# Second attention's filling: half of the output product by seven products of quarters, added straight to the residual rows

## The reference, cut to what matters

```python
def even_layer(h, ..., w_out):
    proj = h @ w_in + b_in
    m_cols, n_cols = jnp.split(proj, [MLSTM_COLS], axis=-1)
    ya = mlstm_branch(m_cols, f_bias, conv_w, conv_b, head_norm)
    yb = nsa_branch(n_cols, q_norm, k_norm, ck_pos, ck_w1, ck_w2, cv_pos, cv_w1, cv_w2)
    return jnp.concatenate([ya, yb], axis=-1) @ w_out
...
    x = x + y.astype(x.dtype)
```

## Time and profile before

| | us |
|---|---|
| median of 3 timed executions | 1676.92 |
| profiled execution, its own time | 1677.36 |
| its span, first to last instruction | 1675.4 |
| TensorE matmuls busy | 1658.8 (99%) |
| VectorE busy | 881.0 (53%) |
| ScalarE busy | 384.7 (23%) |
| GpSimd busy | 205.2 (12%) |

### The profile page before, as it was taken

The page is one execution under the profiler, slowest core; times in us unless marked ns, Lnnn a source line. Parts: engine busy times, 40 slices in busy tenths (PEclk is TensorE's granted clock), DMA queues, the critical chain, the costliest instruction groups (busy, mean ns, idle before and its releaser), DMA issues.

```text
span 1675.4 us, 20036 instructions
## 1 busy us (share of the span) xinstructions
PE 1658.8 (99%) x7754; PEld 1009.6 (60%) x7754; DVE 881.0 (53%) x1497; ACT 384.7 (23%) x690; POOL 205.2 (12%) x267
## 2 busy tenths in 40 slices
PE   9999999999999999999999999999999999999999
PEld 5887888885434343333434456688866654667664
DVE  3755745674523232322325446776756645677663
ACT  3122212002100000010002203331145524544530
POOL 2333410001100000000001000000225510000000
PEclk9999999999999999999999999999999999999999
DMA  7313113245899999999997123213220022212101
GB/s 284 126 57 120 51 51 135 101 175 210 311 422 425 428 426 426 427 427 427 426 428 285 31 104 100 76 58 127 108 101 1 1 76 74 78 50 86 66 1 50
DMA packets 28001, 308.12 MB, mean 184 GB/s; under 512 B 4415, under 2 KB 4703, under 8 KB 10112
## 3 DMA queue, kind: packets, MB, share of 16 engines
q1 hardware_dynamic: 21456, 288.70, 42.6%
q0 software_dynamic: 6448, 18.10, 3.1%
HBM read 306.06 MB, written 4.19 MB: 185 GB/s over the span
## 4 chain that ended last, share of the span: by engine, by line
PE 93%; DVE 3%; DMA 2%; issue 0%; ACT 0%; POOL 0%; DVEq 0%; SPq 0%; ACTq 0%
PE ps L449 89%; PE ps L452 5%; DMA arena<-in_w 2%; DVE arena L1284 2%; DVE arena L1295 0%; POOL small L2967 0%; DVE arena L1311 0%; DVE small L1299 0%; ACT HT L2525 0%; DVE arena L1289 0%; ACT arena L2525 0%; DVE wring L1284 0%; DVE arena L1315 0%; DVE arena L1299 0%; DVE small L1311 0%
## 5 line engine op out<-in xcount | busy, mean ns | idle before, releaser
L449 PE MATMUL ps<-arena 128*64 128x512 f32 (+12 forms) x2484 | 528.4, 394 | 3.6 <-DVE arena L1307 1.2
L449 PEld LDWEIGHTS ps<-arena 128*64 128x64 f32 (+4 forms) x2484 | 251.0, 156 | 219.7 <-issue 208.6
L449 PE MATMUL ps<-wring,arena 128*64 128x512 f32 (+2 forms) x1048 | 345.0, 564 | 0.0
L1284 DVE TENSOR_TENSOR arena<-ps,arena 128x512 f32<-128x512 f32 (+1 forms) x196 | 134.2, 684 | 381.9 <-PE ps L449 229.1
L449 PE MATMUL ps<-wring,HT 128*128 128x512 f32 (+1 forms) x880 | 311.0, 505 | 4.8 <-ACT HT L2525 3.2
L449 PEld LDWEIGHTS ps<-wring,HT 128*128 128x128 f32 x880 | 163.3, 190 | 122.5 <-issue 110.0
L449 PE MATMUL ps<-HT,wring 128*128 128x512 f32 (+2 forms) x656 | 222.1, 501 | 0.0
L2525 ACT ACTIVATE arena<-ps 128x512 f32<-128x512 f32 (+4 forms) x143 | 80.7, 564 | 592.5 <-PE ps L452 303.8
L449 PE MATMUL ps<-wring 128*128 128x256 f32 x864 | 195.8, 380 | 0.0
L449 PEld LDWEIGHTS ps<-wring,arena 128*64 128x64 f32 (+1 forms) x1048 | 131.4, 151 | 87.3 <-issue 82.5
L449 PEld LDWEIGHTS ps<-wring 128*128 128x128 f32 x864 | 162.3, 190 | 24.2 <-issue 2.6
(11 more groups left out here) (125 smaller groups left out, 1002.7 us busy)
## 6 DMA issues: line engine op xcount, KB each, us to landing
wring<-in_w SPq DMA_DIRECT2D x47, 2048.0 KB, 21.3
wring<-in_dense SPq DMA_DIRECT2D x38, 2048.0 KB, 8.3
arena<-in_w SPq DMA_DIRECT2D x35, 2048.0 KB, 20.4
HT<-in_w SPq DMA_DIRECT2D x12, 2048.0 KB, 17.9
arena<-in_rows POOLq DMA_DIRECT2D x29, 256.0 KB, 3.9
wring<-in_dense SPq DMA_DIRECT2D x2, 1024.0 KB, 5.4
H<-in_x SPq DMA_DIRECT2D x4, 512.0 KB, 6.5
arena<-in_relb POOLq DMA_DIRECT2D x8, 256.0 KB, 9.0
```

The source lines that it names most:

```text
L449: return nc.tensor.matmul(o, l, r, start=start, stop=stop, skip_group_check=True)
L1284: done(nc.vector.tensor_tensor(o, a, b, op), tell)
```

## The change

The 16 pieces `e0` go. In their place come 14, named by half of the columns h and product n, in the order of the new table `EIGHTHS` (1, 2, 3, 4, 6, 5, 7): each is one of the seven products of quarters of 256 tokens by 256 inner values by 256 columns, in four matmuls of 256 columns. The quota goes from 0.81 to 0.66 pieces a step; with the 8 pieces `e1` there are 22 pieces instead of 24.

VectorE makes S1 to S4 once (into the space of `y1`, dead by then), behind `nz(6)` and ahead of the loop. For each half h it makes T3 and T2 (`out_sums(h, 3)`), T1 (`out_sums(h, 4)`) and T4 (`out_sums(h, 7)`): T1 and T3 in the place of B11 and B12, T2 and T4 in `kc2`. `out_product` adds each bank to the blocks of `H` that it belongs to: four additions for product 1, one for each other. TensorE waits for `sumw` before products 3 (T2), 4 (T1) and 7 (T4), and for `took` before 6, 5 and 7 (the same bank read before). The wait of a later stage on `suma` goes from 7 to 8, for the one more signal.

```diff
+EIGHTHS = {1: ("a", "A11", "B11"), 2: ("d", "A12", "B21"), 3: ("b", "S2", "T2"), 4: ("c", "S1", "T1"), 6: ("b", "S3", "T3"),
+           5: ("c", "S4", "B22"), 7: ("b", "A22", "T4")}
...
-        FILL_D = softmax_slots([("e0", i, h) for i in range(4) for h in range(2)] + [("e1", i, h) for i in range(4) for h in range(2)],
-                               lambda g: {"e0": 2, "e1": 1}[g[0]], 0.81, NIT + 3, 4)
+        FILL_D = softmax_slots([("e0", h, n) for h in range(2) for n in EIGHTHS] + [("e1", i, h) for i in range(4) for h in range(2)],
+                               lambda g: 1, 0.66, NIT + 3, 4)
...
                     if g[0] == "e0":
-                        _, i, h = g
-                        if p == 0 and i == 0:
+                        _, h, n = g
+                        bank, x, y = EIGHTHS[n]
+                        if n < 5:
+                            f = fill(("e0", h, bank))
+                        if n == 1:
                             weight(f"e_o{h}")
-                        if p == 0 and h == 0:
-                            evacuated(("y1T", i))
-                        out_part(g, i, h, (2 * p, 2 * p + 1), p == 0, p == 1)
+                            for i in range(4):
+                                evacuated(("y1T", i))
+                        if n in (3, 4, 7):
+                            pe.wait_ge(S("sumw"), saw("sumw"))
+                        if n == 3:
+                            pe.wait_ge(S("suma"), 7)
+                        if n in (6, 5, 7):
+                            pe.wait_ge(S("took"), saw("took"))
+                        f, e = F["e0", h, bank], of_output(h)
+                        for s in range(2):
+                            for k in range(2):
+                                ins = mm(f.ap[:, 256 * s:256 * s + 256], e[x][:, k, 128 * s:128 * s + 128], e[y][:, k, :],
+                                         n < 5 and not s and not k, n in (1, 2, 5, 7) and k == 1)
+                        ins.then_inc(f.full if n in (1, 2, 5, 7) else S("seventh"), 1)
...
                 nz(6)
+                e = of_output(0)
+                freed(("y1T", 2))
+                tt(e["S1"], e["A21"], e["A22"], ADD)
+                tt(e["S2"], e["S1"], e["A11"], SUB)
+                tt(e["S3"], e["A11"], e["A21"], SUB)
+                tt(e["S4"], e["A12"], e["S2"], SUB, "suma")
...
+                def out_sums(h, n):
+                    e = of_output(h)
+                    if n == 3:
+                        v.wait_ge(S(f"w{PLACE[f'e_o{h}'][0]}"), 16 * PLACE[f"e_o{h}"][1])
+                        tt(e["T3"], e["B22"], e["B12"], SUB)
+                        tt(e["T2"], e["T3"], e["B11"], ADD, "sumw")
+                    elif n == 4:
+                        tt(e["T1"], e["B22"], e["T2"], SUB, "sumw")
+                    else:
+                        tt(e["T4"], e["B21"], e["T2"], SUB, "sumw")
+
+                def out_product(h, n):
+                    bank = EIGHTHS[n][0]
+                    f = F["e0", h, bank]
+                    if n in (1, 2, 5, 7):
+                        v.wait_ge(f.full, f.at)
+                    else:
+                        heard("seventh")
+                    blocks = {1: ((0, 0), (0, 1), (1, 1), (1, 0)), 2: ((0, 0),), 3: ((0, 1),), 4: ((1, 1),), 6: ((1, 1),),
+                              5: ((0, 1),), 7: ((1, 0),)}[n]
+                    for i, j in blocks:
+                        o = H[:, 2 * i:2 * i + 2, 512 * h + 256 * j:512 * h + 256 * j + 256]
+                        tt(o, f.ap.rearrange("p (s n) -> p s n", s=2), o, ADD,
+                           "v" if (i, j) != blocks[-1] else f if n in (1, 2, 5, 7) else "took")
+                    if n == 1:
+                        if not h:
+                            out_sums(0, 3)
+                        out_sums(h, 4)
+                    elif n == 3:
+                        out_sums(h, 7)
+                    elif n == 7 and not h:
+                        out_sums(1, 3)
+
                 def piece(g, p):
                     if g[0] == "e0":
-                        if p == 1:
-                            h_add(g[1], g[2], full(*g))
+                        out_product(g[1], g[2])
```

More of the change, by code:

```diff
@@ L388, in of_halves, with of_output @@
             return dict(B11=b11, B12=b12, B21=b21, B22=b22, T1=b11, T2=sumw_m, T3=b12, T4=sumw_m)
+        sums_y = y1.rearrange("p (x k n) -> p x k n", x=4, k=2)
+        def of_output(h):
+            (a11, a12), (a21, a22) = [[HT[:, 2 * j:2 * j + 2, 256 * i:256 * i + 256] for j in range(2)] for i in range(2)]
+            w = wslot[PLACE[f"e_o{h}"][0]].rearrange("p (k n) -> p k n", k=8)
+            (b11, b12), (b21, b22) = [[w[:, 2 * i:2 * i + 2, 256 * j:256 * j + 256] for j in range(2)] for i in range(2)]
+            t2 = kc2[:, h, :].rearrange("p (k n) -> p k n", k=2)
+            return dict(A11=a11, A12=a12, A21=a21, A22=a22, B11=b11, B12=b12, B21=b21, B22=b22, T1=b11, T2=t2, T3=b12, T4=t2,
+                        **{f"S{x + 1}": sums_y[:, x] for x in range(4)})
         NORMS = "ABCDE"
@@ L1218, in stage_e @@
                         if (p, n) == (1, 5):
-                            pe.wait_ge(S("suma"), 7)
+                            pe.wait_ge(S("suma"), 8)
                         group(p, n)
```

## The result

The changed kernel takes 1685.82 us (median of 4 runs, 1684.17 to 1686.73), the kernel before in the same job 1676.8 (1676.18 to 1677.49): a ratio of 1.0047, 95% interval 1.0036 to 1.0059. The direction was right, and the time lies in the stated range, 1676 to 1687. The size was not right: the medians differ by 9.0 us, the forecast said 5.3, and 1685.8 is above the forecast case's own range of 1680.3 to 1684.5.

What follows compares the result with a forecast made beforehand. TensorE was taken to bound the loop, with VectorE's in-order queue making it wait: opening 7.5 + middle 1.6 - end 0.2 - saving 3.6 = +5.3 us on 1676.92, thus 1682.2 us, range 1676 to 1687.

Steps and rivals of the forecast that it cites:

- forecast case: Whole kernel: the summed terms, +5.3 us, give 1682.2 us, own range 1680.3 to 1684.5; chance 0.49.
- The opening, step 1: Loop start: S1 to S4 behind `nz(6)` delay `lows(0)`, so `score(1)` waits for its bank; 0.2 us lost.
- Step 2, the wait for T2: Opening: product 3 waits while VectorE does product 1's four additions, T3 and T2; 4.3 us lost.
- Steps 3 and 4: Opening: product 4 waits for product 2's addition, 0.5 us; product 6 for product 3's addition, 2.1 us.
- Step 5: Opening's end: VectorE starts `lows(2)` late, so `score(3)` comes 0.4 us late; opening together 7.5 us.
- The middle: Step 6: product 1's additions and T1 stand ahead of `probs(4)`; 1.6 us lost, bounds 0 to 4.
- The end: Loop end: 0.84 us wait for `yT2` hidden, 0.6 us lost waiting for GpSimd; net 0.2 us gained.
- The saving: TensorE in the loop: 14 new pieces for 16 old ones save 3.6 us, between 2.3 and 4.8.
- Only the opening: Rival: VectorE is ahead at step 6 and the end gains 0.8; +3.1 us, 1680.0 us; chance 0.23.
- All hidden: Rival: VectorE hides all its added work; -4.4 us, 1672.5 us; chance 0.12.
- Weight loads in series: Rival: the added weight loads stand in line, about 10 us more; +15 us, 1692 us; chance 0.01.
- The bared chain: Rival: softmax chain bared too, middle 4 us lost, end 0.4 lost; +8.3 us, 1685.2 us; chance 0.15.

Runs made afterwards that it cites:

- e3: Changed kernel with ten dummy matmuls on TensorE in its three long waits (ahead of products 3 and 6 and step 7's turns): 1684.94 us, ratio 1.0048.
- e7: Changed kernel with all sums but the second half's T1 made ahead of the loop: 1680.15 us, ratio 1.0014 to the kernel before.
- e4: Changed kernel without the twelve sums, plain quarters multiplied instead, the twenty additions and their waits kept: 1680.37 us, ratio 1.0015 to the kernel before.
- e5: Changed kernel with TensorE's part alone: no sums, eight additions in all, no waits for sums or `took`: 1674.71 us, ratio 0.9984 to the kernel before.
- e1: Changed kernel with S1 to S4 made ahead of `nz(6)` instead of behind it: 1682.74 us, ratio 1.0034 to the kernel before.
- e2: Changed kernel with `probs(4)` ahead of product 1's additions in step 6: 1686.24 us, ratio 1.0046 to the kernel before.
- e9: e7 with product 1 added in two operations, its second half split over steps 6 and 8, other additions and `silu_z` reordered: 1678.93 us, ratio 1.0005.
- e6: Changed kernel with eight more VectorE additions of 512 elements in steps 16 to 23, results unused: 1687.39 us, ratio 1.0058 to the kernel before.

## Why the prediction was right in direction and short in size

1. *The opening, step 1:* right. TensorE waited 0.23 us before `score(1)` (0.2 forecast).
2. *Step 2, the wait for T2:* right, 4.36 us for 4.3, and released where I said.
3. *Steps 3 and 4:* the total was mis-sized. `score(2)` came 18.8 us behind `score(0)` where my laid-over times had 18.1. VectorE came to product 3's addition 0.6 us later than in my count: I took 0.04 us between its operations throughout, and where the kind of work changes its timeline has 0.1 or more (1231.48 to 1231.59, 1234.45 to 1234.56). Product 4 also started late, behind a product 3 at half clock, but e3 shows that this cost nothing on top.
4. *Step 5:* 0.83 us before `score(3)` for 0.4, and a further 0.15 before the next turns. In all 9.0 for 7.5.
5. *The middle:* the right place and the right mechanism, the term too small: 2.18 us for 1.6. From its first operation of `lows(6)` to the end of `probs(4)` VectorE took the 6.5 us forecast:

```profile
1265.85 0.69 DVE L1338 COPY arena<-ps 128x512 f32<-128x512 f32 x1
1266.65 0.30 DVE L1311 TENSOR_TENSOR ps<-ps,con 128x124 f32<-128x124 f32 x1
...
1272.45 0.69 DVE L1338 COPY arena<-ps 128x512 f32<-128x512 f32 x1
```

But I had it start 0.1 us behind the scores, and it started 0.7 behind them (TensorE's next work began at 1265.92), still busy with `probs(3)` (the first line): T3 and T2 of the second half had made it late a step earlier, where I had written that the operations fit. TensorE's own way took 5.1 us (to 1271.02) for my 4.9. In e7, with T3 and T2 gone from there, the wait is 1.70 us; in e4, with T1 gone as well, it is 0.98.

6. *The term that was missing altogether* is what a wait does to TensorE's clock. My sum priced a wait at its own length. Behind 4.36 and 2.18 us of idle time the granted clock was 0.50 and 0.61, and a product took 3.1 to 3.55 us for 1.82. In the middle that is 1.7 us on the path (e3 gave them back). In the opening it cost nothing on top (e3). Of the 3.9 us between L's growth and the forecast it is the largest single part; the opening's 1.5 and the middle wait's 0.6 are most of the rest.
7. *The end:* 0.4 gained for 0.2; GpSimd's wait is 0.44 us for 0.6, and that for `yT2` is hidden as forecast.
8. *The saving:* 3.2 us for 3.6 (e5). The new pieces cost 1.82 us at full clock, as the earlier trace rows had it.
9. *The rivals.* Only the opening: out, the step-6 wait is there. All hidden: out, and the experiments say how far off it was; even with nearly all sums outside the loop it wasn't reached (e7). Weight loads in series: out, as eight pairs of a load and a matmul take 1.82 us. The rule of the Trainium skill ("TensorE: Matmul & The Clock Gate", "Part 3: Packing small matmuls — row/col tiling") that a load overlaps only on another row group would have each full-height load stand in line, and doesn't agree with that. The same section also lets a load for the background weight buffer be pulled ahead, which does. The bared chain was numerically nearest (1685.2), but not for its reason: it wanted waits in four or five places behind the opening, and only the one at step 7 is there; between 1290 and 1345 TensorE is busy for 55.00 of 55 us, with no wait. As the top of the stated range came from that rival, it is in part luck that the time lies inside it.

```profile
1290.00:1345.00 55.00, 55.00 (x443) 37.69 (x442) 39.16 (x116) 32.15 (x90) 31.14 (x47) 1.00 0.01 1
```

What stays open: what takes the 0.4 us by which TensorE's saving is short (with 3.2 for 3.6 the terms give 9.3 for 9.2), why the same wait lowers the clock in one kernel's execution and not in another's, and how the opening's loss divides between order and amount.

## What to carry to other kernels

When work moves from the bounding engine to one with idle time, look up the order in which that engine reaches each result that somebody now waits for, and its idle time in each short stretch, not its idle share: here 3 us of TensorE's time was bought with 17.5 us on an engine that idled for 39, but for only 5.8 where 9.8 were added, and it cost 9. A product that needs sums of its operands should have them made ahead of the loop, where VectorE idles and nobody waits for them yet (e7). Price a wait of TensorE of about 2 us at up to twice its length (here 2.18 us and 1.7 behind it), as the clock may fall behind it, and compare the granted clock of the runs before explaining a difference of a few us.

## What the runs showed of the hardware

- *The clock after a short wait.* Low clock (a mean of 0.50 to 0.69 over the next 2.6 to 4.4 us) stood behind waits of 4.36, 2.18, 2.04, 2.03, 2.00 and 1.82 us; full clock (1.00) behind 2.18 (e1), 1.70 (e7), 1.54 (e2) and 1.40 us (e9), and in this loop behind every wait of 1.06 us or less. The same 2.18 us at the same instruction did both, in two kernels. So near 2 us it isn't the wait's length alone that decides.
- *A wait without a name.* The largest wait of all was put down to "issue". A wait on two semaphores (`sumw` and `suma`) had its releaser only in VectorE's timeline, by the end of the operation 0.1 us before.
- *VectorE's spare time* cost TensorE something even though nobody waited for the added result: 0.2 us per us in one trace (e6), in the part of the loop where it was busy 39 of 55 us. Over half of it is two waits for softmax results that came later in VectorE's queue.
